# Feed-forward output products of a two-block transformer kernel: two 256-column products with one weight tile become one of 512 columns

## The reference, cut to what matters

```python
# first block
ff = jnp.einsum('bsf,fd->bsd', jnp.square(jax.nn.relu(...)), w_ff_out[l])   # 4096 -> 1024
x = layer_norm(DEEPNORM_ALPHA * x + (1.0 + g2) * ff, ln2_g[l], ln2_b[l])
# second block, twice in each of two layers
def swiglu_ffn(h, w_in, w_out):
    g, u = jnp.split(h @ w_in, 2, axis=-1)
    return (jax.nn.silu(g) * u) @ w_out                                      # 2816 -> 1024
x = x + 0.5 * swiglu_ffn(rms_norm_2(x, ffn1_norm[i]), ffn1_w_in[i], ffn1_w_out[i])
```

## Time and profile before

| what | us |
|---|---|
| time, median of 3 runs (lowest, highest) | 1604.79 (1603.89, 1605.89) |
| span of the profiled execution, first to last instruction | 1602.3 |
| PE busy, PEld busy in the span | 1548.0, 1515.4 |
| DVE busy, ACT busy, POOL busy | 1067.1, 835.1, 171.2 |
| mean granted TensorE clock | 0.993 |

### The profile page before, as it was taken

How to read it: one execution, slowest core, us unless ns; L and a number is a source line. 1 busy time by engine, 2 the same in 40 slices (tenths; PEclk the granted TensorE clock), 3 DMA queues, 4 the chain that set the end, 5 groups by cost and what they waited for, 6 DMA issues and landing times.

```text
span 1602.3 us, 31666 instructions
## 1 busy us (share of the span) xinstructions
PE 1548.0 (97%) x12977; PEld 1515.4 (95%) x12977; DVE 1067.1 (67%) x1557; ACT 835.1 (52%) x1210; POOL 171.2 (11%) x223
## 2 busy tenths in 40 slices
PE   6999999999999999999999999999999999999998
PEld 6899989999998999999999999999998889999998
DVE  7887877886656666575666557665656676566653
ACT  6566546755545444564544454444465555454442
POOL 2013200400113500010100000000100111000000
PEclk9999999999999999999999999999999999999999
DMA  9653963465553554562454565555653014355553
GB/s 381 262 198 107 350 253 132 158 244 185 201 191 115 210 200 164 189 231 96 175 205 176 173 207 197 193 169 185 234 192 132 27 65 173 106 181 187 182 174 116
DMA packets 45126, 293.14 MB, mean 183 GB/s; under 512 B 5201, under 2 KB 6497, under 8 KB 15713
## 3 DMA queue, kind: packets, MB, share of 16 engines
q1 hardware_dynamic: 41184, 265.49, 46.4%
q0 software_dynamic: 3840, 26.23, 4.2%
HBM read 288.02 MB, written 3.67 MB: 182 GB/s over the span
## 4 chain that ended last, share of the span: by engine, by line
PE 77%; DVE 11%; ACT 6%; DMA 4%; issue 2%; DVEq 0%; POOL 0%; SPq 0%; ACTq 0%
PE G L449 23%; PE G L451 22%; PE G L450 22%; DVE w_lo L1636 4%; ACT w_hi L1087 3%; PE O L668 3%; PE L L1048 1%; PE T L654 1%; DMA mod_x<-w_ada 1%; DMA raw<-w_xv 1%; PE L L917 1%; DVE X L1762 1%; DMA raw<-w_wouta 1%; ACT x_hi L1170 1%; DMA raw<-w_f1in 1%
## 5 line engine op out<-in xcount | busy, mean ns | idle before, releaser
L1636 DVE TENSOR_TENSOR w_lo<-raw,w_hi 128x2048 fp32r<-128x2048 f32 (+1 forms) x256 | 541.4, 2118 | 262.8 <-ACT w_hi L1087 262.2
L449 PE MATMUL G<-x_hi,w_hi 128*128 128x256 f32 (+1 forms) x2183 | 611.9, 280 | 12.6 <-DVE w_lo L1636 7.9
L450 PE MATMUL G<-x_lo,w_hi 128*128 128x256 f32 (+1 forms) x2183 | 607.0, 278 | 0.0
L451 PE MATMUL G<-x_hi,w_lo 128*128 128x256 f32 (+1 forms) x2183 | 606.9, 278 | 0.0
L1087 ACT ACTIVATE w_hi<-raw 128x2048 fp32r<-128x2048 f32 (+1 forms) x260 | 458.9, 1768 | 150.1 <-DMA raw<-w_ffout 35.3
L449 PEld LDWEIGHTS G<-x_hi,w_hi 128*128 128x128 f32 (+1 forms) x2183 | 412.0, 189 | 18.9 <-DVE w_lo L1636 9.5
L450 PEld LDWEIGHTS G<-x_lo,w_hi 128*128 128x128 f32 (+1 forms) x2183 | 412.2, 189 | 0.1
L451 PEld LDWEIGHTS G<-x_hi,w_lo 128*128 128x128 f32 (+1 forms) x2183 | 411.8, 189 | 0.1
L449 PE MATMUL G<-hid_hi,w_hi 128*128 128x256 f32 x1280 | 360.7, 282 | 2.9 <-DVE hid_lo L1668 2.3
L451 PE MATMUL G<-hid_hi,w_lo 128*128 128x256 f32 x1280 | 356.7, 279 | 0.0
L450 PE MATMUL G<-hid_lo,w_hi 128*128 128x256 f32 x1280 | 356.6, 279 | 0.0
(11 more groups left out here) (420 smaller groups left out, 1873.3 us busy)
## 6 DMA issues: line engine op xcount, KB each, us to landing
raw<-w_f1in SPq DMA_DIRECT2D x44, 1024.0 KB, 4.8
raw<-w_f2in SPq DMA_DIRECT2D x44, 1024.0 KB, 4.7
raw<-w_f1out SPq DMA_DIRECT2D x32, 704.0 KB, 4.1
raw<-w_f2out SPq DMA_DIRECT2D x32, 704.0 KB, 4.0
raw<-w_ffin SPq DMA_DIRECT2D x16, 1024.0 KB, 4.8
raw<-w_ffout SPq DMA_DIRECT2D x16, 1024.0 KB, 4.8
mod_x<-w_ada POOLq DMA_DIRECT2D x12, 1024.0 KB, 8.5
mod_w<-w_ada POOLq DMA_DIRECT2D x8, 1024.0 KB, 12.0
```

The lines of the kernel that those rows point to most:

```text
L449: mm(out, l_hi, r_hi, start=start, stop=False)
L450: mm(out, l_hi, r_lo, start=False, stop=False)
L451: return mm(out, l_lo, r_hi, start=False, stop=stop)
L1636: v.tensor_tensor(w_lo[b][:, 0:s.size], raw[b][:, 0:s.size], w_hi[b][:, 0:s.size].bitcast(F32), ALU.subtract).then_inc(s_lo, 1)
```

## The change

`hid_hi` and `hid_lo` become two halves of one tensor, at the same addresses. The five output stages call `gemm_wide` in place of `gemm_a`: for each chunk the high weight tile is multiplied by high and low units at once (512 moving columns, two runs of 256), so that high by high lands in the left half of the bank and high by low in the right half; the low weight by the high units (256 columns) goes on into the left half. At the tile's end DVE adds first the right half, then the left half, to `X`, both scaled alike. The first addition is wrapped in `own`.

```diff
-        hid_hi = place("hid_hi", [P, 32, S], F32R, 0)
-        hid_lo = place("hid_lo", [P, 32, S], F32R, 32)
+        hid_two = place("hid_two", [P, 2, 32, S], F32R, 0)
+        hid_hi, hid_lo = hid_two[:, 0], hid_two[:, 1]
...
+            def gemm_wide(s, slot, j, x_two, kn, k0, start, stop, i=0, between=None):
+
+                n = s.n0 + slot
+                slot_begins(s, slot, j if start else None, i, 2)
+                wh = w_hi[n % RING][:, 0:kn * P].rearrange("p (k c) -> p k c", k=kn)
+                wl = w_lo[n % RING][:, 0:kn * P].rearrange("p (k c) -> p k c", k=kn)
+                for k in range(kn):
+                    if between and k == 1:
+                        between()
+                    mm(G[j % 2][:, :], wh[:, k, :], x_two[:, :, k0 + k, :], start=start and k == 0, stop=False)
+                    last = mm(G[j % 2][:, 0:S], wl[:, k, :], x_two[:, 0, k0 + k, :], start=False,
+                              stop=stop and k == kn - 1)
+                last.then_inc(s_mm, 1)
...
-                        gemm_a(s, 2 * g + part, s.j0 + g, hid_hi, hid_lo, kn=kn, nf=1, k0=part * kn,
-                               start=part == 0, stop=part == 1, i=i, groups=2)
+                        gemm_wide(s, 2 * g + part, s.j0 + g, hid_two, kn, part * kn, part == 0, part == 1, i)
...
                 result(s, g * per + per - 1)
+                if nf == 1:
+                    own(v.scalar_tensor_tensor(X[:, g, :], G[j % 2][:, S:2 * S], mod1[:, gate0 + g:gate0 + g + 1],
+                                               X[:, g, :], ALU.mult, ALU.add))
...
+                    if nf == 1:
+                        own(v.scalar_tensor_tensor(X[:, g, :], G[j % 2][:, S:2 * S], factor, X[:, g, :],
+                                                   ALU.mult, ALU.add))
```

## The result

The changed kernel is **slower by 0.67%**: 1617.75 us against 1607.18 us for the kernel before, medians of 20 runs each taken in turns, ratio 1.0067 with a 95% interval of 1.0048 to 1.0086, that is 7.7 to 13.8 us. The forecast was 6.9 us faster. Rival 5, the slow pace in every output stage, is what happened.

A forecast was written before the change was run, and what follows sets the result against it. The number and pace of PE's products were taken to bound the kernel. Gains of 4.1 and 3.9 less 0.46, 0.46 and 0.15 made 6.9 us, from 1604.8 to 1597.9 us; range 1588 to 1608.

The forecast's parts named there:

- Rival 5: Output stages: slow pace spreads to fast ffout, f1out0, f1out1 and excess goes by columns; 9.0 us slower, 1613.8; chance 0.12.
- the price of the wide product: PE, output stages: excess counted once per product, 220 ns fast; steps 333.3 and 342.2 ns, gaining 4.1 and 3.9 us.
- rival 4: Output stages: nothing per product, excess is a rate of the moving stream; steps stay 340 and 353.4 ns; 1605.7; chance 0.21.
- The float32 rows: Profile rows of plain float32 products, taken as showing a cost per product: four of 512 columns at 427.5 ns each.
- rival 2: Every output stage: wide and narrow pair costs 327 ns per step, as in plain float32; 1588.7 us; chance 0.10.
- my own case: Output stages: the forecast itself, excess per product; 1597.9 us, own range 1594 to 1600; chance 0.45.
- would cost 342.2: Objection to the slow pace spreading: with a gain per product a slow step costs 342.2 ns, so the loss nearly vanishes.
- the jump of 32 KiB: Wide product: its two runs of moving columns lie 32 KiB apart, a mix that might settle in the slow pace.
- the stage ends: Ends of output stages: added addition costs 0.46 us in f2out1 and in f1out0; ffout 0; f2out0 and f1out1 hidden.
- removed loads: PE, output stages: 960 weight loads fewer, worth nothing by themselves since the streams cover them.
- The additions: DVE: one more per tile, 40 in all, 0.42 us plus 0.04 us hand-over each; hidden inside stages.
- The 0.15 us of lost gain: End of f1out0: splits start from slots loaded earlier, so the last two slots' gain is lost, 0.15 us.

The follow-up runs named there:

- runs 13 to 17: Changed kernel with one 512-column product per output stage, three products of 256 elsewhere; five executions of in effect one kernel: 1605.56, 1611.67, 1607.70, 1612.81 and 1620.22 us.
- runs 7 and 10: Changed kernel with 16-bit operands, columns 4 bytes apart: 7 reads the upper halves of the same words, 1601.12 us; 10 a constant tile, 1597.33 us.
- run 9: Changed kernel with 16-bit weights and constant 16-bit moving columns side by side, hidden units left out: 1593.27 us.
- run 2: Changed kernel with the wide product on 512 neighbouring columns, without the jump from high to low units: 1614.54 us, one run.
- run 3: Changed kernel with three products of 256 columns per step, two fed from two runs of 128: 1614.76 us, ratio 1.0053 to the kernel before.
- runs 1, 5, 13: Changed kernel with the wide product cut into two of 256 (1, 1607.57 us), kept in every second chunk (5, 1615.35), or once per stage (13, 1605.56).
- runs 13 to 18: Changed kernel with single wide products among products of 256: one per output stage in 13 to 17, one per weight slot in 18 (1619.79 us).

## Why the prediction was wrong

**The step that failed** is the price of the wide product: "the excess belongs to the product", 213.3 + 6.7 = 220 ns, and 224.4 in the slow stages. Measured is 235, and 353.3 ns a step where 333.3 and 342.2 were forecast. Two things are in it.

- *The excess goes by columns.* A single wide product in a fast stream takes 226 ns, twice 113.3, and not 220 (runs 13 to 17). In 16-bit form two products cost the 340 ns of three (runs 7 and 10), and 15 ns of that go with the columns' distance of 4 bytes (run 9). This is rival 4's mechanism. Its rate, 340 / 768, is 0.443 ns a column. The float32 rows on which the forecast leaned show a cost per product at half the rate of columns, and say nothing of what columns cost at the full rate; I had put that down as the objection to rival 2 and not used it against my own case.
- *A wide product ends the fast pace.* This is rival 5. With rival 4 alone the change would have cost 0.9 us. I gave it 0.12 since nothing in the trace picked the pace, and thought the forecast would protect even then, as a slow step "would cost 342.2". The two readings weren't independent: with the excess going by columns (0.21 + 0.12 by my own chances) the slow pace was the only thing left to decide. Its condition was half right: the jump of 32 KiB isn't needed (run 2) and doesn't force the slow pace (run 3), the width does (runs 1, 5, 13). And something in the trace did show where the pace changes, if not which it takes: the stall behind the first slot, at which both slow stages turned.

**The size.** The kernel before has a fast stage in 2 of 4 for `ffout` and 10 of 16 for the others: 256 x 1/2 + 704 x 10/16 = 568 steps that would be fast and now cost 13.3 ns more, 7.6 us. With 0.9 us at the stage ends that is 8.5 us, an estimate from twenty stages; measured are 10.6, 7.7 to 13.8. What makes up the other 2 us, if it is not chance, no run shows. In the two traces, from first to last start: `ffout` loses 3.4 us, `f1out0` and `f1out1` 2.2 each, together 7.7 (608 x 13.3 would be 8.1), `f2out0` and `f2out1` nothing. That the spans differ by only 2.3 us comes mostly from ahead of the change: PE came to `ffout` at 399.6 where it had been 404.4. Of these 4.7 us, 3.1 are two waits of PE for other engines that were longer in the kernel before. The larger one, there:

```profile
223.75 0.49 PE L804 MATMUL L<-kz,qz 128*128 128x128 f32 x2 [2.84 <-ACT V L1112]
```

In the later trace that wait is 0.69 us.

**The steps that held:**

- Columns unchanged, 960 products and loads fewer, and removed loads worth nothing by themselves.
- The additions: 0.42 + 0.03 us where 0.42 + 0.04 was put. Inside the stages hidden; no wait for `w_lo` or a bank shows there.
- The ends: `f1out0` +0.46 (1.09 to 1.55 us), `f2out1` +0.46 (0.63 to 1.09), `f2out0` hidden with 1.5 us left. In `ffout` PE waits 2.04 us in place of 2.51: the addition is hidden, and the DMA on the chain, which starts behind the stage's last product in both, took 4.70 us in place of 5.14. The 0.15 us of lost gain in `f1out0` has no gain to be lost from.
- That two paces exist, and how to read them from starts.

**What stays open.** What picks the pace of a stream of 256-column products behind a stall; why a wide product turned five of seven slow streams fast that had their slow pace from elsewhere (runs 13 to 18), and none of the 69 that had it from an earlier wide product; whether a jump inside a product makes the slow pace more frequent (run 3); and how the load takes part. No kernel here that does the whole computation holds the fast pace through or beats the kernel before.

## What to carry to other kernels

Joining products saves nothing where the moving stream is bound by its columns, and that can often be read beforehand: compare the distance of starts at two widths *of the same type*; if only another type has them, treat the excess as going by columns. Where one code shows two paces, a change of shape may settle which one it gets, and here the worse one cost more than the change could bring; weigh that case by how many stages now have the better pace (three of five in this profile). And judge such a kernel over many runs: the two profiled executions here differ by 2.3 us, the medians by 10.6.

## What the runs showed of the hardware that was not expected

- TensorE streams float32r in one of two paces at the same full clock, 113.3 or 117.8 ns for 256 columns, holds it over whole stages and across code, and changes it at stalls. A single 512-column product changes it without one: fast to slow in 20 of 20 stages of runs 13 to 17.
- The distance of moving columns in memory costs time: 16-bit columns 4 bytes apart take 226 ns for 512, side by side 216. A step of 768 columns goes from 340 to 325 ns.
- A wide float32r product costs 235 ns in a stream with others of its kind, more than two of 256 at the fast pace (226.7), and as much as two at the slow one (235.6). A single one in a fast stream costs 226.
